# Grouped mixture of experts on one Trainium2 core: the down-projection in one plain fp32 pass instead of three passes on split operands

## What is computed

```python
scores = jax.nn.sigmoid((t @ w_router).astype(jnp.float32))
...
combine = jnp.sum(jax.nn.one_hot(e_idx, N_EXPERTS, dtype=jnp.float32) * w[..., None], axis=1).astype(t.dtype)
out = jnp.zeros_like(t)
for e in range(N_EXPERTS):
    h_e = jax.nn.silu(t @ w_gate[e]) * (t @ w_up[e])
    out = out + combine[:, e:e + 1] * (h_e @ w_down[e])
```

## Time and profile before

| | us |
|---|---|
| median of 3 runs | 2367.61 |
| lowest and highest run | 2358.72, 2368.34 |
| span of the profiled execution, first to last instruction | 2365.3 |
| TensorE busy in it | 2088.0 |
| VectorE busy | 1140.7 |
| ScalarE busy | 778.9 |
| GpSimd busy | 754.8 |

### The profile page before, as it was taken

One profiled execution on the slowest core, in us unless ns is written; L12 is line 12 of the kernel. 1 busy time (PEld: TensorE's weight loads), 2 busy tenths in 40 slices (PEclk: granted clock), 3 DMA queues, 4 the chain that ended last, 5 costly groups with the idle time before them and its releaser, 6 DMA issues.

```text
span 2365.3 us, 21135 instructions
## 1 busy us (share of the span) xinstructions
PE 2088.0 (88%) x7788; PEld 1311.7 (55%) x7788; DVE 1140.7 (48%) x1560; ACT 778.9 (33%) x892; POOL 754.8 (32%) x276
## 2 busy tenths in 40 slices
PE   8998987899899998989899979978899788888886
PEld 1223455554444436777777745555558566666664
DVE  0002456615631126666666643552561376766664
ACT  1002222212410014555555532221230265555553
POOL 0000034412000004656566630141300076666663
PEclk9999999998999998999999999999899999999998
DMA  9882211041012222665555632211302456655661
GB/s 370 313 289 97 97 36 36 1 104 39 1 36 71 78 100 73 214 212 213 213 213 213 213 112 103 72 36 49 94 8 100 178 209 229 236 214 213 214 217 51
DMA packets 160809, 329.02 MB, mean 139 GB/s; under 512 B 21072, under 2 KB 22224, under 8 KB 160720
## 3 DMA queue, kind: packets, MB, share of 16 engines
q1 hardware_dynamic: 143312, 323.66, 38.5%
q10 hardware_dynamic: 17408, 4.20, 1.1%
HBM read 326.79 MB, written 1.05 MB: 139 GB/s over the span
## 4 chain that ended last, share of the span: by engine, by line
PE 66%; DVE 20%; issue 6%; ACT 5%; POOL 2%; DMA 0%; PEldq 0%; DVEq 0%; ACTq 0%; SPq 0%; POOLq 0%
PE bank L369 18%; PE bank L333 7%; PE bank L380 5%; PE bank L612 4%; PE bank L555 4%; PE bank L543 3%; DVE ring_lo L1557 3%; DVE pick L1536 3%; ACT w_hi L1037 3%; PE bank L686 3%; DVE pickw L1540 3%; PE bank L651 2%; PE bank L660 2%; PE bank L646 2%; PE bank L717 2%
## 5 line engine op out<-in xcount | busy, mean ns | idle before, releaser
L1170 POOL TENSOR_TENSOR ring_lo<-ring,w_hi 128x2048 fp32r<-128x2048 f32 (+1 forms) x96 | 586.7, 6122 | 883.9 <-ACT w_hi L1037 883.9
L369 PE MATMUL bank<-hT,ring 128*128 128x512 f32 (+1 forms) x1280 | 472.1, 525 | 13.4 <-DVE hT L1252 12.7
L369 PEld LDWEIGHTS bank<-hT,ring 128*128 128x128 f32 x1280 | 244.5, 193 | 225.2 <-issue 202.6
L1037 ACT ACTIVATE w_hi<-ring 128x4096 fp32r<-128x4096 f32 x96 | 347.6, 3620 | 14.0 <-PEq L289 14.0
L1557 DVE TENSOR_TENSOR ring_lo<-ring,w_hi 128x2048 fp32r<-128x2048 f32 (+1 forms) x96 | 235.0, 2448 | 125.7 <-ACT w_hi L1037 125.6
L1127 POOL TENSOR_TENSOR dec<-pf 128x512 f32<-128x512 f32 (+1 forms) x32 | 28.0, 875 | 551.1 <-DVE pb L1292 433.3
L686 PE MATMUL bank<-ring_lo,picked_hi 128*128 128x512 f32 x512 | 139.6, 417 | 50.6 <-POOL ring_lo L1170 28.0
L333 PE MATMUL bank<-ring,cond 128*2 128x512 f32 x384 | 170.6, 598 | 10.8 <-DMA ring<-in_w_ada 10.8
L1260 DVE SCALAR_TENSOR_TENSOR xT<-bank,mod,xT 128x256 f32<-128x256 f32 x216 | 97.6, 481 | 149.1 <-PE bank L555 73.8
L686 PEld LDWEIGHTS bank<-ring_lo,picked_hi 128*128 128x128 f32 x512 | 96.1, 196 | 88.5 <-POOL ring_lo L1170 41.8
L612 PE MATMUL bank<-hrow_hi,pick 128*128 128x512 f32 x192 | 97.1, 506 | 53.4 <-DVE pickw L1540 53.4
(11 more groups left out here) (205 smaller groups left out, 2934.3 us busy)
## 6 DMA issues: line engine op xcount, KB each, us to landing
ring<-in_w_gate SPq DMA_DIRECT2D x32, 2048.0 KB, 8.4
ring<-in_w_up SPq DMA_DIRECT2D x32, 2048.0 KB, 9.1
ring<-in_w_down SPq DMA_DIRECT2D x32, 2048.0 KB, 7.8
ring<-in_w_ada SPq DMA_DIRECT2D x24, 2048.0 KB, 8.9
ring<-in_w_in SPq DMA_DIRECT2D x24, 2048.0 KB, 8.1
ring<-in_w_out SPq DMA_DIRECT2D x4, 2048.0 KB, 10.4
ring<-in_w_na_o SPq DMA_DIRECT2D x2, 2048.0 KB, 7.6
bias_skew<-in_rel_bias_reversed ACTq DMA_DIRECT2D x64, 64.0 KB, 3.8
```

The source lines that it names most:

```text
L369: mm = T.matmul(o[:, lo:TOK], w[:, k, c * P:(c + 1) * P], hT[:, k, lo:TOK], start=(k == 0), stop=(k == KT - 1))
L1037: S.activation(w_hi[m % 2][:], ring[:, s, :], ACT.Copy).then_inc(sem["w_hi_ready"], 1)
L1170: G.tensor_tensor(ring_lo[:, s, a], ring[:, s, a], w_hi[(3 * e + g) % 2][:, a].bitcast(f32), ALU.subtract).then_inc(sem["w_lo_ready"], 1)
```

## The change

The down-projection takes the slab as it lies in `ring`, in fp32, and the activations as one fp32 tile `acts_t`, in one pass of 8 matmuls. So the down slab is neither copied nor subtracted, `acts_hi` and `acts_lo` become `acts_t`, and TensorE waits for the slab's load itself. Gate slabs now always use the first `w_hi` buffer and up slabs the second. On ScalarE the copy of the next gate slab stands directly behind silu. On TensorE the next expert's rows are turned after the whole projection.

The diff, cut to its core:

```diff
@@ TensorE, down
-                        hi = w_hi[(3 * e + 2) % 2][:].rearrange("p (k n) -> p k n", k=4)
-                        low = ring_lo[:, (base + 3 * e + 2) % SLOTS, :].rearrange("p (k n) -> p k n", k=4)
-                        pe.wait_ge(*total(ph, i, "w_hi_ready", e, 3))
-                        pe.wait_ge(*total(ph, i, "acts_hi_ready", e, 1))
+                        m = base + 3 * e + 2
+                        w = ring[:, m % SLOTS, :].rearrange("p (k n) -> p k n", k=4)
+                        full_at = 16 * (m // SLOTS + 1)
+                        pe.wait_ge(slot_full[m % SLOTS], full_at if i is None else i * 48 + full_at)
+                        pe.wait_ge(*total(ph, i, "acts_t_ready", e, 1))
...
                             for k in range(4):
-                                T.matmul(bank[6 + half][:, :], acts_hi[:, k, :], hi[:, k, half * 512:(half + 1) * 512],
-                                         start=(k == 0), stop=False)
-                        pe.wait_ge(*total(ph, i, "acts_lo_ready", e, 1))
-                        for half in range(2):
-                            for k in range(4):
-                                T.matmul(bank[6 + half][:, :], acts_lo[:, k, :], hi[:, k, half * 512:(half + 1) * 512],
-                                         start=False, stop=False)
+                                mm = T.matmul(bank[6 + half][:, :], acts_t[:, k, :], w[:, k, half * 512:(half + 1) * 512],
+                                              start=(k == 0), stop=(k == 3))
+                            mm.then_inc(sem["y_done"], 1)
                         if not last:
                             turn_rows(i, e + 1)
-
-                        pe.wait_ge(*total(ph, i, "w_lo_ready", e, 3))
-                        pe.wait_ge(*total(ph, i, "own_lo_ready", e, 3))
-                        for half in range(2):
-                            for k in range(4):
-                                mm = T.matmul(bank[6 + half][:, :], acts_hi[:, k, :],
-                                              low[:, k, half * 512:(half + 1) * 512], start=False, stop=(k == 3))
-                            mm.then_inc(sem["y_done"], 1)
@@ ScalarE, split_high and expert
-                        name, k = (("gate_done", 1), ("up_done", 1), ("y_done", 2))[(m - 2) % 3]
-                        act.wait_ge(*total(ph, i, name, (m - 2) // 3, k))
-                        S.activation(w_hi[m % 2][:], ring[:, s, :], ACT.Copy).then_inc(sem["w_hi_ready"], 1)
+                        act.wait_ge(*total(ph, i, ("gate_done", "up_done")[g], e - 1, 1))
+                        S.activation(w_hi[g][:], ring[:, s, :], ACT.Copy).then_inc(sem["w_hi_ready"], 1)
...
                         S.activation(silu[:], bank[0][:, :], ACT.Silu).then_inc(sem["silu_ready"], 1)
-                        split_high(i, e, 2)
+                        if not last:
+                            split_high(i, e + 1, 0)
                         act.wait_ge(*total(ph, i, "act_turned", e, 1))
                         act.wait_ge(*total(ph, i, "y_done", e - 1, 2))
-                        S.activation(acts_hi[:].rearrange("p k c -> p (k c)"), bank[5][:, :], ACT.Copy)\
-                            .then_inc(sem["acts_hi_ready"], 1)
+                        S.activation(acts_t[:].rearrange("p k c -> p (k c)"), bank[5][:, :], ACT.Copy)\
+                            .then_inc(sem["acts_t_ready"], 1)
                         if not last:
-                            split_high(i, e + 1, 0)
                             keep_rows(i, e + 1)
@@ GpSimd, expert
-                        split_low(i, e, 2)
@@ VectorE, expert
-                        split_low(i, e, 2)
-                        dve.wait_ge(*total(ph, i, "acts_hi_ready", e, 1))
-                        V.tensor_tensor(acts_lo[:].rearrange("p k c -> p (k c)"), bank[5][:, :],
-                                        acts_hi[:].rearrange("p k c -> p (k c)").bitcast(f32),
-                                        ALU.subtract).then_inc(sem["acts_lo_ready"], 1)
```

More of the change, by code:

```diff
@@ L176, in build @@
     acts = fixed("acts", [P, FF], offset=A0 + 94 * KB)
-    acts_hi = fixed("acts_hi", [P, 4, P], f32r, offset=A0 + 96 * KB)
-    acts_lo = fixed("acts_lo", [P, 4, P], f32r, offset=A0 + 98 * KB)
+    acts_t = fixed("acts_t", [P, 4, P], offset=A0 + 96 * KB)
     unused = fixed("unused", [P, TOK], offset=A0 + 100 * KB)
@@ L190, in build @@
         hrow_hi_ready hrow_ready gathered pickw_turned gate_done up_done act_turned rows_turned y_done scattered
-        pick_bare pick_ready spread_ready act_ready acts_lo_ready picked_lo_ready y_lo_ready x_added own_lo_ready
-        rows_ready picked_hi_ready slot_weight_ready silu_ready acts_hi_ready y_hi_ready w_hi_ready w_lo_ready
+        pick_bare pick_ready spread_ready act_ready picked_lo_ready y_lo_ready x_added own_lo_ready
+        rows_ready picked_hi_ready slot_weight_ready silu_ready acts_t_ready y_hi_ready w_hi_ready w_lo_ready
         dve_chain act_chain pool_chain pool_ready""".split()
@@ L252, in build @@
                    "rows_turned": 2, "y_done": 2, "scattered": 4,
-                   "pick_bare": 1, "pick_ready": 1, "spread_ready": 1, "act_ready": 1, "acts_lo_ready": 1,
-                   "picked_lo_ready": 2, "y_lo_ready": 2, "x_added": 4, "own_lo_ready": 3,
+                   "pick_bare": 1, "pick_ready": 1, "spread_ready": 1, "act_ready": 1,
+                   "picked_lo_ready": 2, "y_lo_ready": 2, "x_added": 4, "own_lo_ready": 2,
                    "rows_ready": 2, "picked_hi_ready": 2, "slot_weight_ready": 1, "silu_ready": 1,
-                   "acts_hi_ready": 1, "y_hi_ready": 2, "w_hi_ready": 3, "w_lo_ready": 3}
+                   "acts_t_ready": 1, "y_hi_ready": 2, "w_hi_ready": 2, "w_lo_ready": 2}
         signalled_by = {
             "pe": ("gathered", "pickw_turned", "gate_done", "up_done", "act_turned", "rows_turned", "y_done", "scattered"),
-            "dve": ("pick_bare", "pick_ready", "spread_ready", "act_ready", "acts_lo_ready", "picked_lo_ready",
+            "dve": ("pick_bare", "pick_ready", "spread_ready", "act_ready", "picked_lo_ready",
                     "y_lo_ready", "x_added", "own_lo_ready"),
-            "act": ("rows_ready", "picked_hi_ready", "slot_weight_ready", "silu_ready", "acts_hi_ready", "y_hi_ready",
+            "act": ("rows_ready", "picked_hi_ready", "slot_weight_ready", "silu_ready", "acts_t_ready", "y_hi_ready",
                     "w_hi_ready"),
@@ L282, in by_fours @@
                 body(None, e, e == count - 1)
-        gpsimd_part = (SLOT * 3 // 4, SLOT // 2, SLOT // 2)
+        gpsimd_part = (SLOT * 3 // 4, SLOT // 2)
         def open_phase(engine, who):
@@ L697, in expert @@
                         else:
-                            pe.wait_ge(*total(ph, i, "acts_lo_ready", e - 1, 1))
+                            pe.wait_ge(*total(ph, i, "acts_t_ready", e - 1, 1))
                         for j in range(4):
```

6 lines of the change are left out of this document (3 added, 3 removed).

## The result

| | us |
|---|---|
| before, median of 4 runs | 2367.98 (2358.72 to 2371.39) |
| after, median of 4 runs | 2519.31 (2515.88 to 2520.95) |
| ratio, 95% interval | 1.0643 (1.062 to 1.0665) |
| profiled execution after: its time, its span | 2520.95, 2519.1 |
| forecast | 2517 |

The account below looks back on a forecast made before the run. TensorE was nearly the bound, losing 55 and 68 us to waits. Seven even halves, seven odd halves and a last half per layer gave +87 and +62, together +149 us on 2365.3: 2517 us as median, range 2420 to 2555.

Parts of the forecast that it names:

- even half: Stretch after an even expert, TensorE going straight on: pickw waits behind GpSimd's gate share, +4.9 us in either layer.
- odd half: Stretch after an odd expert, where TensorE first scatters two experts: +7.3 us in layer 0, +3.7 us in layer 1.
- last half of layer 0: Each layer's last even half, with no next expert to pick for, meets only the later up copy: +2 us.
- (1) The stream.: TensorE's down-projection: 8 fp32 matmuls take 6.87 us where three passes took 5.58, +1.3 us for each of 32 experts.
- (2) The turned rows.: Rows turned after the projection: TensorE waits about 0.45 us for picked_hi; up copy starts 2.6 us after it, not 0.5.
- (3) The freed engines.: Down slab's copy and subtractions and acts_lo go; on the path only GpSimd's share matters (4.45 us unblocked), since pickw waited.
- (4) The gate copy.: Gate copy behind silu: GpSimd's 3072-wide share holds the port 6.7 us ahead of pickw, pick or VectorE's up share.
- TensorE's stream only: Rival, chance 0.10: gate share's wait equals the down share's, odd halves absorb the rest; +56 us, 2423 us.
- The port goes to VectorE: Rival, chance 0.08: pickw gets the port ahead of GpSimd's gate share in even halves; sum -14 us, 2353 us.
- All waits go: Rival, chance 0.04: time freed on GpSimd and ScalarE removes every TensorE wait of both expert stages; -67 us, 2300 us.
- upper bound: Top of the forecast case, 2555 us: four full fp32 passes (+18) and longer half-rate stretches after longer gaps (+20).

Follow-up runs that it names:

- the one with the stream alone: The kernel before, with only the down-projection's three passes replaced by 8 fp32 matmuls on the high parts, all copies, subtractions and waits kept: 2402.8 us, ratio 1.0151.
- the kernel with three moves: The changed kernel with gate copy behind the activations' copy, rows turned between the projection's halves, up copy ahead of picked_hi: 2276.27 us, best of the study.
- the three single edits: The changed kernel with, each alone, gate copy back behind the turned activations (2322.1 us), pick and pickw made earlier (2367.97), rows turned between projection halves (2380.48).

## Why the prediction was right

The time came within 3 us of the forecast. So close a hit is in part luck: in sum the steps were off by up to 5 us, in both directions, and this nearly cancels. Here they are, measured from the starts of ScalarE's copies of y. The timeline of ScalarE after, at experts 0, 14 and 15 of each layer (T is 1.47 us before the start of a row of two; for the last expert it is the start of its last row):

```profile
945.98 1.10 ACT L1066 ACTIVATE y_hi<-bank 128x512 fp32r<-128x512 f32 x2
...
1447.38 1.10 ACT L1066 ACTIVATE y_hi<-bank 128x512 fp32r<-128x512 f32 x2
...
1471.89 0.60 ACT L1066 ACTIVATE y_hi<-bank 128x512 fp32r<-128x512 f32 x1 [2.78 <-PE bank L646]
...
2463.78 1.10 ACT L1066 ACTIVATE y_hi<-bank 128x512 fp32r<-128x512 f32 x2
...
2490.76 0.60 ACT L1066 ACTIVATE y_hi<-bank 128x512 fp32r<-128x512 f32 x1 [2.78 <-PE bank L646]
```

and before, at experts 0 and 14 of layer 0:

```profile
944.47 0.60 ACT L1079 ACTIVATE y_hi<-bank 128x512 fp32r<-128x512 f32 x1 [0.28 <-PE bank L660]
...
1363.99 0.60 ACT L1079 ACTIVATE y_hi<-bank 128x512 fp32r<-128x512 f32 x1 [0.28 <-PE bank L660]
```

From expert 0 to 14 lie seven even and seven odd halves: 501.4 us after, 419.5 before, 81.9 more. The same marks one by one (seven differences each) give the table; in layer 1 the fourteen halves took 61.8 us more.

| | forecast | measured |
|---|---|---|
| layer 0, even half | +4.9 | +5.0 |
| layer 0, odd half | +7.3 | +6.7 |
| layer 1, even half | +4.9 | +4.9 |
| layer 1, odd half | +3.7 | +4.0 |
| last half of layer 0, of layer 1 | +2, +2 | +3.7, +5.6 |

- **(1) The stream.** Right: 7.03 us for 8 matmuls, 6.87 from start to start; alone it cost 36 us where 32 x 1.3 is 42. By the four passes that the Trainium skill counts (FP8 and Floating Point Precision, "TensorE Precision Notes") an estimate gave 7.44 us, four times the 1.86 of a pass on split data; the trace has 3.7 times.
- **(2) The turned rows.** Right: TensorE waits 0.40 us for `picked_hi` (0.45 said), 31 times, and the up copy starts at T+2.4 (2.6 said).
- **(3) The freed engines.** Right: only GpSimd's share was on the path, and where nothing takes its place its removal is a gain. The run with the gate copy moved back is 81 us faster than the one with the stream alone, with the down share gone and nothing in its place before `pickw`.
- **(4) The gate copy.** Right in mechanism and size. Gate copies start 8.2 to 9.6 us after T (8.6 said), `pickw` lasts 7.0 us in the even halves of layer 0 and 6.7 to 6.8 in those of layer 1 (6 to 7.5 said), `pick` 6.95 in layer 1's odd halves (6 to 7). VectorE's up share in layer 0's odd halves takes 5.64 to 7.02 us (5 to 6 said), longer than said in four of seven. The gaps of TensorE are 4.0 to 5.5, 3.1 to 4.4, and 4.6 to 4.8 us (6, 3.5 and 5 said).
- **The last halves** were too small: the +2 forgot the longer projection of the last expert itself (1.3 us each), and the lower clock, which it had not counted there: the third pass before it took 3.67 us in layer 0 and 3.01 in layer 1 for some 2.13, and in layer 1 the projection itself 9.79 for 7.03 (below). That is 5 us in all, and layer 1's odd halves were 2 us too small in sum; against it layer 0's odd halves were 4 us too dear (0.6 each, seven times). This is the luck in the sum.
- **The rivals.** *TensorE's stream only* would be 56 us; the waits did not trade evenly, since the new blocker is half as long again. *The port goes to VectorE* names the right point: it is what happened when the rows were turned earlier, where `pickw` won by 0.46 us. *All waits go* described no part of the changed kernel, but three moves of two engines' instructions go past its 2300: TensorE is idle for 31 us in the two stages there, where it was 124 before.

The sum of the causes, roughly: TensorE's listed waits grew from 104 to 179 us (+75), the stream added 36, and some 40 us of the 151 are left. They are longer instructions at the lower of the two clocks. TensorE's busy time in the two stages grew by 81 us, twice what the longer stream asks, while the granted clock fell. In the kernel with three moves the same 3425 matmul records are busy for 826 us at a clock of 0.99, in the changed kernel for 907 at 0.92 and 0.87. The shares can't be priced by undoing one thing at a time: the three single edits gave back 197, 151 and 139 us, each alone, because each takes the same victims out of the way.

## What to carry to other kernels

When work is removed from an engine, ask first what the remaining work will now collide with. Here the subtraction that was dropped held a shared port before a critical operation for 4.45 us, and the one that a copy's new place put there holds it for 6.7. Where two engines exclude each other, compare the moment at which each is ready: here `pickw` came 0.46 us ahead in one run and 1.3 us behind in another, and that decided a wait of 4.0 to 5.5 us for TensorE in the even halves of layer 0. The order to look for is long port users under the stretches where nobody on the path wants the port; once that was reached here, their length was free (2276.27 and 2276.26 us).

## What was not expected of the hardware

- **The same wait in front of the third pass lowered the clock at some places and not at others.** In the changed kernel GpSimd's up share holds TensorE for 2.13 to 2.21 us in every even half. The 8 matmuls behind that take 2.13 us at 1101.48, near the 2.02 of the 2.4 GHz level in the earlier trace rows, and 3.63 one pair later, at 1172.31. They are slow in four of eight such halves of layer 0 and in seven of eight of layer 1. A slow pass there costs little, since the gather waits for `pickw` in any case: in layer 0 the gap after it is 4.0 us instead of 5.5. With the rows turned between the halves of the projection (alone, or with the late gate copy) the wait is 1.71 to 1.74 us, and none of the 32 passes behind it is slow. The timeline of TensorE in the changed kernel, layer 0, then the last expert of layer 1:

```profile
1172.31 3.63 PE L674 MATMUL bank<-ring_lo,picked_hi 128*128 128x512 f32 x8 [2.17 <-POOL ring_lo L1157]
...
2475.17 3.01 PE L674 MATMUL bank<-ring_lo,picked_hi 128*128 128x512 f32 x8 [2.13 <-POOL ring_lo L1157]
2479.08 1.11 PE L688 MATMUL bank<-const,acts 128*128 128x128 f32 x4 [0.90 <-DVE acts L1557]
2480.93 9.79 PE L646 MATMUL bank<-ring,acts_t 128*128 128x512 f32 x16 [0.73 <-issue]
```

  In the last expert there are three waits in 6 us, none above 2.2, and part of the projection runs at 1.2 GHz. What tells the places apart was not tried.
- **The stretch at half rate did not grow with the gap.** After 5.5 us idle the gather matmuls last 0.63 us from 1109.72 and 0.39 from 1114.32, some 5 us, as after 3.4 us idle in the earlier trace rows. The upper bound's "longer stretch at half rate after longer gaps" did not occur there.
- **A blocked instruction reads as a busy one.** `pickw` shows 6.98, 4.82 or 0.69 us for the same work, and VectorE is "busy" for 305 us in the changed kernel's experts of layer 0, and for 233 in the best kernel's, which do the same work (288 instructions in both). Such an engine looks like a bound until the same operation's shortest row is set beside it.
